# Gated linear attention in a two-block forward pass: outputs of both directions added up in PSUM, state updates scaled on ScalarE

## What is computed

```python
def step(s, xs):                      # one chunk of one direction
    qc, kc, vc, ac = xs
    b = jnp.cumsum(ac, axis=2)
    diff = b[:, :, :, None, :] - b[:, :, None, :, :]
    decay = jnp.exp(jnp.where(mask, diff, -jnp.inf))
    attn = jnp.einsum('bhid,bhjd,bhijd->bhij', qc, kc, decay)
    o = jnp.einsum('bhid,bhde->bhie', qc * jnp.exp(b), s) + jnp.einsum('bhij,bhje->bhie', attn, vc)
    b_last = b[:, :, -1:, :]
    s_new = jnp.exp(b_last[:, :, 0, :])[..., None] * s + jnp.einsum(
        'bhjd,bhje->bhde', kc * jnp.exp(b_last - b), vc)
    return s_new, o
...
return o_f + flip(o_b), s_f, s_b      # bidir_scan
...
y = o * lax.rsqrt(jnp.mean(o * o, axis=-1, keepdims=True) + NORM_EPS) * g_norm
return from_heads(y) * jax.nn.silu(gate)
```

## Time and profile before

| | us |
|---|---|
| median of 3 runs | 2616.42 |
| lowest and highest | 2613.99, 2625.62 |
| the profiled execution's own time | 2624.51 |
| its span (first to last instruction) | 2622.7 |
| TensorE matmul busy, share of the span | 2347.3, 89% |
| VectorE busy | 1414.9, 54% |
| ScalarE busy | 589.8, 22% |
| GpSimd busy | 1107.8, 42% |
| mean granted TensorE clock, share of full speed | 0.937 |

### The profile page before, as it was taken

How to read it: one execution, slowest core, us unless ns; L and a number is a source line. 1 busy time by engine, 2 the same in 40 slices (tenths; PEclk the granted TensorE clock), 3 DMA queues, 4 the chain that set the end, 5 groups by cost and what they waited for, 6 DMA issues and landing times.

```text
span 2622.7 us, 34114 instructions
## 1 busy us (share of the span) xinstructions
PE 2347.3 (89%) x14068; PEld 1874.8 (71%) x14068; DVE 1414.9 (54%) x2005; ACT 589.8 (22%) x1159; POOL 1107.8 (42%) x632
## 2 busy tenths in 40 slices
PE   7998799999799996999998788968678897899998
PEld 5867588888477774788886265956577885688886
DVE  5455547346833346457456543877945583550531
ACT  2042221121222232220221220302533221210210
POOL 4613267666342214567664130613210034466653
PEclk9999899999899998999999799968879998999999
DMA  4201134335221101235236110212110002223321
GB/s 158 92 30 41 41 98 152 127 97 178 79 76 41 41 25 64 72 105 180 93 113 229 74 48 8 66 32 73 41 49 3 3 2 72 64 89 97 105 90 63
DMA packets 54059, 204.12 MB, mean 78 GB/s; under 512 B 6001, under 2 KB 6129, under 8 KB 52881
## 3 DMA queue, kind: packets, MB, share of 16 engines
q1 hardware_dynamic: 52560, 188.34, 22.0%
q0 software_dynamic: 1344, 13.60, 1.3%
HBM read 197.72 MB, written 4.19 MB: 77 GB/s over the span
## 4 chain that ended last, share of the span: by engine, by line
PE 79%; DVE 15%; ACT 3%; issue 1%; POOL 1%; DMA 0%; DVEq 0%; SPq 0%; POOLq 0%; ACTq 0%
PE bank L493 59%; PE bank L781 3%; PE bank L809 2%; PE bank L610 1%; DVE nb L619 1%; PE bank L1339 1%; PE bank L1359 1%; PE bank L796 1%; PE bank L2022 1%; PE bank L1367 1%; DVE nb L1911 1%; PE bank L2018 1%; PE bank L785 1%; DVE big L1902 1%; POOL parts_r L484 1%
## 5 line engine op out<-in xcount | busy, mean ns | idle before, releaser
L493 PE MATMUL bank<-xn_r,parts_r 128*128 128x512 f32 (+1 forms) x3104 | 980.6, 394 | 44.0 <-DVE big_r L504 13.2
L493 PE MATMUL bank<-big_r,parts_r 128*128 128x512 f32 x3112 | 901.5, 393 | 1.0 <-POOL parts_r L484 1.0
L482 POOL TENSOR_SCALAR parts_r<-ring 128x1024 fp32r<-128x1024 f32 x297 | 334.6, 1127 | 1232.1 <-PE bank L493 1207.4
L484 POOL TENSOR_TENSOR parts_r<-ring,parts_r 128x1024 fp32r<-128x1024 f32 x297 | 748.6, 2521 | 24.8
L493 PEld LDWEIGHTS bank<-xn_r,parts_r 128*128 128x128 f32 x3104 | 592.6, 193 | 172.1 <-issue 41.8
L493 PEld LDWEIGHTS bank<-big_r,parts_r 128*128 128x128 f32 x3112 | 585.0, 189 | 124.3 <-DVE big_r L504 2.7
L740 DVE SCALAR_TENSOR_TENSOR big<-bank,small,big 128x511 f32<-128x511 f32 x88 | 65.9, 749 | 277.1 <-ACT big L719 277.1
L719 ACT ACTIVATE big<-bank,small 128x512 f32<-128x512 f32 x88 | 68.3, 781 | 497.2 <-PE bank L493 497.2
L2372 DVE SCALAR_TENSOR_TENSOR h<-bank,vecs,h 128x512 f32<-128x512 f32 x24 | 17.8, 750 | 193.5 <-PE bank L493 193.5
L2418 DVE TENSOR_TENSOR big<-big 128x512 f32<-128x512 f32 x32 | 82.3, 2573 | 70.4 <-ACT big_r L2399 70.4
L493 PE MATMUL bank<-parts_r,xn_r 128*128 128x384 f32 x352 | 92.1, 343 | 11.7 <-DVE big L1902 9.5
(11 more groups left out here) (348 smaller groups left out, 2983.2 us busy)
## 6 DMA issues: line engine op xcount, KB each, us to landing
ring<-weights SPq DMA_DIRECT2D x297, 512.0 KB, 3.5
cst<-mod_w SPq DMA_DIRECT2D x48, 512.0 KB, 3.8
big<-consts POOLq DMA_DIRECT2D x1, 4096.0 KB, 15.9
cst<-consts SPq DMA_DIRECT2D x2, 1280.0 KB, 8.2
h<-x SPq DMA_DIRECT2D x8, 256.0 KB, 5.7
h_store<-h POOLq DMA_DIRECT2D x1, 2048.0 KB, 7.8
h<-h_store POOLq DMA_DIRECT2D x1, 2048.0 KB, 9.0
out<-mix SPq DMA_DIRECT2D x8, 256.0 KB, 2.2
```

The lines of the kernel that those rows point to most:

```text
L482: pool.tensor_scalar(rounded(w_hi[:, slot]), w, 1.0, 0.0, ALU.mult, ALU.add).then_inc(sem("hi_ready"), 1)
L484: pool.tensor_tensor(rounded(w_lo[:, slot]), w, value(w_hi[:, slot]), ALU.subtract).then_inc(part_ready, 1)
L493: mm = pe.matmul(ps, rounded(w[a]), rounded(x[b]), start=(start and n == 0), stop=(stop and n == 2))
```

## The change

Seven edits, all within the GLA branch:

1. Outputs stay in PSUM. Banks 4 to 7 hold all of them from the first score block to the close: `gl_out` gives each token block and head its place, token blocks 1 and 2 in banks 4 and 5, blocks 0 and 3 in 6 and 7. The first product into a bank has `start=True`; everything after adds to it, over both directions. The copies to `gl_o` (L1680) and the additions (L1713) are gone.
2. VectorE no longer waits for a block's product before the next block's masks, which use two scratch tiles in turn.
3. ScalarE scales the updates, one instruction of 96 columns for each direction and half (four to a step), into two buffers `gl_U` in turn. The last step's update, which nothing reads, is left out: eleven instead of twelve.
4. VectorE's state update is four instructions of 96 columns, each multiply and add in one; the first is a copy. `gl_Sr` has two buffers.
5. TensorE forms updates two steps ahead: `update(0)` and `update(1)`, then in step n `cross(n)` and `update(n + 2)`.
6. The gain is multiplied into `gate` by GpSimd (`gla_gate_pool`), between the units of `gl_g` and those of `gd_q`.
7. The close is in two halves, banks 4 and 5 and then 6 and 7 (`gla_close_act`, `gla_close_dve`). ScalarE squares from PSUM, VectorE sums, takes the reciprocal, multiplies out of PSUM by it, and by the gate.

The core of the diff:

```diff
             def inner(tb):
                 pe.wait_ge(*after("gl_A", tb + 1))
-                ps = grab(pe, 4 + tb % 2, *after("gl_in", tb + 1))
                 for hd in range(GH):
-                    mm = pe.matmul(ps[:, hd * GLA_DV:(hd + 1) * GLA_DV], gl_A[:, tb % 2, hd * P:(hd + 1) * P],
-                                   gl_v[:, CB + tb, hd * GLA_DV:(hd + 1) * GLA_DV], start=True, stop=True)
+                    mm = pe.matmul(gl_out(tb, hd), gl_A[:, tb % 2, hd * P:(hd + 1) * P],
+                                   gl_v[:, CB + tb, hd * GLA_DV:(hd + 1) * GLA_DV],
+                                   start=(hd < 2 and tb in (OUTS[0][0], OUTS[1][0])), stop=False)
...
+            def cross(n):
+                for d in range(2):
+                    c = steps(d)[n] - CCH
+                    r = CH * (c % 2)
+                    pe.wait_ge(sem("gl_Sr"), 2 * (n - CCH) + d + 1)
+                    for hd in (0, 2, 1, 3):
+                        q, dc = 64 * (hd % 2), 2 * d + hd // 2
+                        mm = pe.matmul(gl_out(c // 2, hd, slice(r, r + CH)), gl_q1[q:q + 64, dc, c * CH:(c + 1) * CH],
+                                       gl_Sr[(n - CCH) % 2][q:q + 64, dc, :], start=False,
+                                       stop=(hd >= 2 and n in last_cross))
+                    mm.then_inc(sem("gl_x"), 1)
...
+            update(0)
+            update(1)
+            for n in range(NCH):
                 if n >= CCH:
...
+                    cross(n)
+                if n + 2 < NCH - 1:
+                    update(n + 2)
...
+            for n in range(NCH - 1):
+                act.wait_ge(*after("gl_U", n + 1))
+                if n >= 2:
+                    act.wait_ge(*after("gl_S", n - 1))
+                for dc in range(4):
+                    c = steps(dc // 2)[n]
+                    ins = act.activation(gl_U[n % 2][:, dc], bank[2 * (n % 2) + dc // 2][:, (dc % 2) * GLA_DV:(dc % 2 + 1) * GLA_DV],
+                                         ACT.Copy, scale=gl_sc[:, 2, dc * NCH + c:dc * NCH + c + 1])
+                ins.then_inc(sem("gl_u"), 1)
...
+                dve.wait_ge(*after("gl_u", n + 1))
...
+                    for dc in range(4):
+                        c = steps(dc // 2)[n]
+                        ins = dve.scalar_tensor_tensor(out=gl_S[:, dc], in0=gl_S[:, dc],
+                                                       scalar=gl_sc[:, 1, dc * NCH + c:dc * NCH + c + 1],
+                                                       in1=gl_U[n % 2][:, dc], op0=ALU.mult, op1=ALU.add)
...
+        def gla_gate_pool(pool):
+            g = gate.rearrange("p b (h n) -> p (b h) n", h=GH)
+            pool.wait_ge(*after("gla_gate", TB))
+            pool.tensor_tensor(g, g, small_cols("gla_ng", GLA_DV).unsqueeze(1).broadcast_to((P, 4 * TB, GLA_DV)), ALU.mult)\
+                .then_inc(sem("gla_gate_scaled"), 1)
...
+                for hh in range(2):
+                    act.activation(gl_sqr[:, 2 * p + hh], bank[4 + 2 * p + hh][:, 0:GW], ACT.Square).then_inc(sem("gla_squared"), 1)
+                act.wait_ge(*after("gla_ss", p + 1))
+                act.activation(stat[:, 8 * p:8 * p + 8], stat[:, 8 * p:8 * p + 8], ACT.Sqrt).then_inc(sem("gla_sd"), 1)
```

More of the change, by code:

```diff
@@ L1597, in steps @@
             return list(range(NCH)) if d == 0 else list(range(CCH))[::-1] + list(range(CCH, NCH))[::-1]
+        last_cross = [CCH + max(2 * max(pair) + 1, 2 * TB - 1 - 2 * min(pair)) for pair in OUTS]
         def gla_pe(pe):
@@ L1603, in gla_pe @@
             for b in range(NBLK):
[L1604 removed]
+                ps = grab(pe, 2 + b % 2, *after("glkT", b + 1))
                 for dc in range(4):
@@ L1645, in gla_pe @@
                 mm.then_inc(sem("gl_U"), 1)
-                if n >= CCH:
[L1647 to L1658, removed]
+            def cross(n):
[9 more added lines that the diff above has]
+                    mm.then_inc(sem("gl_x"), 1)
+            scores(0)
+            for b in range(4, 8):
+                grab(pe, b, *after("gla_normed", 1))
+            for tb in range(TB):
+                if tb + 1 < TB:
+                    scores(tb + 1)
+                inner(tb)
+            pe.wait_ge(*after("glkT", NBLK))
+            update(0)
+            update(1)
+            for n in range(NCH):
+                if n >= CCH:
+                    cross(n)
+                if n + 2 < NCH - 1:
+                    update(n + 2)
         def gla_act(act):
@@ L1696, in gla_dve @@
-                for d in range(2):
-                    c = steps(d)[n]
-                    S, u = gl_S[:, 2 * d:2 * d + 2], gl_U[:, 2 * d:2 * d + 2]
-                    dve.tensor_tensor(S, S, scol(1, d, c), ALU.mult)
-                    U = bank[2 * (n % 2) + d][:, 0:2 * GLA_DV].rearrange("p (a n) -> p a n", a=2)
-                    ins = dve.tensor_tensor(u, U, scol(2, d, c), ALU.mult)
-                ins.then_inc(sem("gl_Su"), 1)
-                dve.wait_ge(*after("gl_Su", n + 1))
-                link(dve, dve.tensor_tensor(gl_S[:, :], gl_S[:, :], gl_U[:, :], ALU.add))
@@ L1705, in gla_dve @@
-                if n >= CCH:
-                    for d in range(2):
-                        c = steps(d)[n] - CCH
-                        r = CH * (c % 2)
-                        dve.wait_ge(*after("gl_x", 2 * (n - CCH) + d + 1))
-                        for hh in range(2):
-                            o = v4(gl_o[r:r + CH, c // 2])[:, hh::2]
-                            x_ = bank[4 + 2 * d + hh][r:r + CH, 0:2 * GLA_DV].rearrange("p (a n) -> p a n", a=2)
-                            dve.tensor_tensor(o, o, x_, ALU.add).then_inc(sem("gl_add"), 1)
-                        dve.wait_ge(*after("gl_add", 4 * (n - CCH) + 2 * d + 2))
+                        dve.tensor_tensor(gl_Sr[m % 2][:, 2 * d:2 * d + 2], gl_S[:, 2 * d:2 * d + 2],
+                                          scol(0, d, steps(d)[n]), ALU.mult).then_inc(sem("gl_Sr"), 1)
@@ L2467, in block2_dve @@
             gla_dve(dve)
-            heads_dve(dve, "gla", gl_o, gate, "gla_gate", gl_res, "gla_ng")
+            gla_close_dve(dve)
             delta_in_dve(dve)
```

101 lines of the change are left out of this document (68 added, 33 removed).

## The result

| | before | after |
|---|---|---|
| median of 16 runs each, us | 2625.28 | 2602.22 |
| lowest run, us | 2613.99 | 2593.38 |
| ratio of the times, 95% interval | | 0.9927 (0.9906 to 0.9948) |
| the profiled execution, us | 2624.51 | 2611.72 |
| its span, us | 2622.7 | 2609.9 |

A forecast was written before the change was run, and what follows sets the result against it. VectorE was taken to set the branch's pace, with the next projection waiting for the branch. 2.8 + 1.8 + 18.0 + 1.7 = 24.3 us off the 2616.42 median of three gives 2592.1 us, range 2584 to 2603.

The forecast's parts named there:

- score blocks: Up to the branch's last score product: 4.6 us less, of which GpSimd takes back 1.8, so -2.8 us.
- context steps: From the last score product to the first scaled state: 6.5 us instead of 8.3, ScalarE slowest, -1.8 us.
- latent steps: Eight steps before the close: 1.70 us each instead of 3.81, VectorE still the bound, narrowly; -18.0 us.
- close: Branch's end before its transposes: two halves, 7.7 us of VectorE, plus 0.2 us for ScalarE's copy and table load; -1.7 us.
- next projection starts: Right behind the branch's transposes, before at 1785.72: all branch savings arrive there, 24.3 us, with L493 near 1761.
- The circle without a hold: Score blocks before GpSimd's interference: VectorE 2.2 and TensorE 2.7 us a block, last product at 1730.0, 4.6 us less.
- The collision: Score blocks: GpSimd's work falls on the adds of blocks 0 and 1; one collision taken, block 1's, 1.8 us.
- the sign: Score blocks: one add of line 1707 was to last 2 to 3 us.
- Neither rival: Latent steps: the round trip, chance 0.16, total 2597; or adding matmuls that cannot overlap, chance 0.03, total 2632.
- the round trip: Latent steps: the circle through TensorE and ScalarE closes every two steps, 2.25 us a step, 19.5 saved; chance 0.16.
- the added products: Latent steps: matmuls adding into filled banks might not overlap, a step 6.6 us, 16 us slower than before; chance 0.03.
- all four numbers: Latent step times: VectorE 1.70, TensorE 1.55, ScalarE 1.1, round trip 1.5 us; claimed within 0.2 us of each other.

The follow-up runs named there:

- gain later: Changed kernel with GpSimd's gain multiply placed two gd_q units later; 2600.79 us (5 runs, ratio 0.9898) and 2600.93 us (12 runs, 0.9900).
- one close: Changed kernel with the early half of the close undone: squares of banks 4 and 5 wait for the last product of all; 2613.24 us, ratio 0.9943.
- the kernel with both moves: Changed kernel with the gain's multiply two units later and scores of blocks 0 and 1 ahead of the key transposes; 2602.26 us, ratio 0.9904.

## Right and wrong, by the prediction's steps

In us, from the two profiles, by times from the start of each span:

| term | predicted | measured |
|---|---|---|
| score blocks, to the last product | -2.8 | +1.0 |
| context steps | -1.8 | -1.9 |
| latent steps | -18.0 | -17.5 |
| close | -1.7 | -2.3 |
| next projection starts | -24.3 | -20.6 |

The stages ahead of the branch ended 0.5 us later in the changed kernel's profile. Counted from the last gate copy, as in the table of the experiments, the first line is +0.5 and the last -21.2.

**Score blocks: the step that failed.** The term was -2.8 and came out as +1.0. The circle without a hold was right. It gave -4.6, and with the gain later the blocks end 4.65 us sooner (17.18 against 21.83). The collision was in the right place, but on both adds instead of one, and cheap: no add lasted the 2 to 3 us that I had named as the sign, and from the first transpose it takes 17.64 us with it and 16.55 without (one close, gain later), 1.1 instead of 1.8. What the sum left out is the clock. I had read 0.91 for this window and taken 1.13 and 1.71 us for granted, "TensorE needs 2.7" a block. A hold of 1.8 us on the path keeps TensorE waiting for as long, and I priced that as time passing, not as idleness of TensorE. 2.7 became 5.0. The prediction looked at what the clock might give back in the steps, where TensorE has slack either way, and not at what it could take in the blocks, where it has none. The last product, which was to end near 1732, ended at 1735.69; the first scaled state came at 1742.05 instead of 1738, and L493 at 1765.08 instead of 1761.

With the clock at 1.00 the same term would have been too careful, not too bold: in the one close profile the blocks end 4.9 us sooner than before (16.94 against 21.83). So the sum for the branch came within 4 us in part by luck: 5.4 us lost to the clock stand against 2.1 us that the term had missed here and 0.6 in the close.

**A term I didn't see** goes the other way. The gain's multiply waits for the gate, so GpSimd stood still for 5.12 us ahead of it, and in that time VectorE finished the keys sooner. VectorE's last step for the keys, in the timeline of before and of after:

```profile
1703.73 9.65 DVE L1592 TENSOR_TENSOR big<-big 128x768 f32<-128x768 f32 x4
```

```profile
1704.27 6.61 DVE L1599 TENSOR_TENSOR big<-big 128x768 f32<-128x768 f32 x4
```

These four read two SBUF tiles, as the adds do, and took 3 us less. The transposes no longer wait for them, and start 0.7 us ahead of the gate copy's end rather than 0.6 behind it, 1.3 us gained. All profiles with the gain in its place show 6.6, all others 9.65. The Trainium skill (SBUF — State Buffer, Who interferes with whom) has VectorE instructions with two SBUF inputs contend with GpSimd's reads; this case agrees at both places, here for the gain and in the score blocks against it.

**Context steps: right.** 6.36 us against the 6.5 worked out; ScalarE paces them, at 0.27 a copy.

**Latent steps: right in kind, 0.07 a step off.** VectorE is the bound, 0.63 + 1.00 and 0.14 of waits instead of 0.07. Neither rival came: VectorE never waits for another engine (the round trip is there only with edit 5 undone), and the added products are spaced 0.05 us apart at the lower clock, as before, and 0.03 to 0.04 after the clock rose at 1748.5, which left the step at 1.77. The prediction held for the round trip that all four numbers lie within 0.2 us of each other. They don't by its own sum: 1.70, 1.55 and 1.5 do, ScalarE's 1.1 doesn't.

**Close: right, 0.6 too careful.** Each half takes 3.65 us of VectorE, and ScalarE's table load (1.28 us, at 1752.03) is done before VectorE's last pair, where I had put 0.2 us. (The close before has five instructions of 1.76 us, not six; the sum used its length and not their number.) The early half is worth 1.7 us, I had said 1.5.

**The total.** The branch gave 20.6 us to the profiled execution, its span 12.8. Of the missing 7.8, 7.1 lie in one later stage that the change doesn't touch, the recurrence of the delta rule. The windows from its first to its last product, before, after, and in the last profile of the changed kernel:

```profile
2099.50:2161.10 61.60, 59.12 (x639) 52.92 (x640) 50.00 (x92) 17.58 (x65) 19.48 (x23) 1.00 0.01 2
```

```profile
2079.70:2148.40 68.70, 68.03 (x639) 61.83 (x640) 50.57 (x92) 17.59 (x65) 19.35 (x23) 0.83 0.00 1
```

```profile
2081.40:2169.90 88.50, 88.17 (x639) 80.20 (x640) 51.27 (x93) 17.54 (x65) 19.66 (x24) 0.62 0.00 1
```

61.6 us at 1.00, 68.7 at 0.83, 88.5 at 0.62, the same instructions. The third profile of the changed kernel took 83.5 at 0.66, so one program draws very different lengths here from one execution to the next. Only one profile is of the kernel before, so whether the change moves this stage on average isn't shown by the profiles; the ratio of the times says 19 us (14 to 25), and the branch 20.6. For the profiled execution the sum gave 2600.2 us and 2611.72 came: 3.7 us of that is the branch, 7.8 the other stages. For the median, the start from three runs was the weak point, 8.9 us, where I had taken 4 us for its movement.

## What to carry to other kernels

When an edit makes a busy TensorE wait once for a microsecond or two, price the stage behind it at both clocks: here the longer wait cost 1.1 us and the lower clock behind it 5.4. Before helper work is put on GpSimd, list what VectorE does with two SBUF inputs while it runs and while it waits. A hold of 1.8 us was free as soon as TensorE had other work in front of the product that needed the add, so the order of TensorE's queue is another cure. Of the versions tried, the gain two units later is the simplest, and its branch is 5.5 us shorter than that of the changed kernel, which the whole times are too scattered to show.

## What the runs showed of the hardware that I had not expected

- Products of a block at 0.50 of the clock took 2.02 us against 1.13, scores 3.09 against 1.71: 1.8 times, where the clock's factor is 2. The steps that VectorE paced stayed at 1.77 us at either clock.
- Idle time of 1.9 us in TensorE, after 6.8 us of transposes and scores, was followed by the lower clock in five of six profiles, and of 2.71 us in the one that had it. The Trainium skill (TensorE: Matmul & The Clock Gate, HAM oscillation — how this bites in real kernels) describes a kernel whose waits for transfers, between short bursts of matmuls, let the clock drop again and again. The rows agree on the kind; the waits that it describes are longer than the 1.9 us here.
- The mean granted clock goes with nearly the whole scatter of this kernel. Over the 16 runs of the changed kernel time and clock correlate at -0.99, with 19.5 us for each 0.01 of mean clock (2593.38 us at 0.944, 2633.17 at 0.925).
- GpSimd's 1536-column multiply took 2.92 us, not 1.5 times the 2.36 of 1024 columns; in the kernel with both moves, where VectorE's adds run beside it, it took 3.44 us.
